# Attention values as the stationary operand, in two column halves of the array, with units handled in pairs

## What is computed

```python
# group A, for a block of 128 queries
s = (jnp.einsum('bqhd,bshd->bhqs', qn, k_nope)
     + jnp.einsum('bqhd,bsd->bhqs', qr, k_rope)).astype(jnp.float32) * scale
mask = (qp[:, None] // CHUNK) >= k_chunk[None, :]
s = jnp.where(mask[None, None], s, -jnp.inf)
p = jax.nn.softmax(s, axis=-1).astype(v.dtype)
return jnp.einsum('bhqs,bshd->bqhd', p, v)
...
# group B: the same with the keys of the top 256 of
rel = jax.nn.relu(jnp.einsum('bqhd,bsd->bqhs', iqb, ik).astype(jnp.float32))
score = jnp.einsum('bqh,bqhs->bqs', iwb.astype(jnp.float32) * w_scale, rel)
```

## Time and profile before

| | us |
|---|---|
| median of 3 runs | 4346.73 |
| lowest and highest | 4341.33, 4348.23 |
| profiled execution, its own time | 4354.86 |
| its span | 4352.8 |
| TensorE busy | 3868.6 (89%) |
| TensorE weight loads busy | 3113.4 (72%) |
| VectorE busy | 2261.7 (52%) |
| ScalarE busy | 1636.0 (38%) |
| GpSimd busy | 1351.6 (31%) |
| mean granted TensorE clock | 0.938 of full speed |

### The profile page before, as it was taken

One profiled execution on the slowest core, in us unless ns is written; L12 is line 12 of the kernel. 1 busy time (PEld: TensorE's weight loads), 2 busy tenths in 40 slices (PEclk: granted clock), 3 DMA queues, 4 the chain that ended last, 5 costly groups with the idle time before them and its releaser, 6 DMA issues. The chain is left out here.

```text
span 4352.8 us, 57519 instructions
## 1 busy us (share of the span) xinstructions
PE 3868.6 (89%) x20100; PEld 3113.4 (72%) x20100; DVE 2261.7 (52%) x4226; ACT 1636.0 (38%) x2907; POOL 1351.6 (31%) x845
## 2 busy tenths in 40 slices
PE   7999977778889899999895589699999999999998
PEld 5777744666677677777783467588878878879986
DVE  3222223899999898889942533244044224404421
ACT  3333323545556556555451222233133223213321
POOL 0000001555555455553001000144444444434332
PEclk9999988789999999899997689899999999999999
DMA  4222222101000000000001045533343433434331
GB/s 165 72 86 81 74 67 56 47 27 30 22 23 19 16 19 17 9 17 11 12 6 47 3 177 183 186 89 115 126 117 95 150 115 92 128 116 116 87 100 61
DMA packets 347675, 323.98 MB, mean 74 GB/s; under 512 B 52928, under 2 KB 284960, under 8 KB 347488
## 3 DMA queue, kind: packets, MB, share of 16 engines
q1 hardware_dynamic: 335360, 277.61, 21.7%
q10 hardware_dynamic: 7344, 26.74, 1.5%
q0 software_dynamic: 4800, 17.43, 1.0%
HBM read 251.54 MB, written 71.43 MB: 74 GB/s over the span
## 5 line engine op out<-in xcount | busy, mean ns | idle before, releaser
L1494 POOL TENSOR_TENSOR ff_w_lo<-ff_stage,ff_w_hi 128x2048 fp32r<-128x2048 f32 (+1 forms) x136 | 611.0, 4493 | 1212.6 <-ACT ff_w_hi L1576 1212.6
L2082 DVE TENSOR_SCALAR_CACHE_REDUCE at_hit<-at_score,at_su 128x384 bf16<-128x384 f32 (+13 forms) x434 | 641.1, 1477 | 8.6
L95 PE MATMUL ff_bank<-ff_h_hi,ff_w_hi 128*128 128x512 f32 (+1 forms) x1760 | 618.7, 352 | 29.7 <-DMA ff_h_lo<-scr_h2T 26.1
L96 PE MATMUL ff_bank<-ff_h_lo,ff_w_hi 128*128 128x512 f32 (+1 forms) x1760 | 620.4, 353 | 0.0
L97 PE MATMUL ff_bank<-ff_h_hi,ff_w_lo 128*128 128x512 f32 (+1 forms) x1760 | 619.2, 352 | 0.0
L1638 DVE TENSOR_TENSOR ff_a_lo<-ff_prod,ff_a_hi 128x512 f32 (+1 forms) x110 | 411.9, 3745 | 170.6 <-ACT ff_a_hi L1590 170.6
L1947 ACT ACTIVATE at_probt<-at_p_t 128x512 f32<-128x512 f32 (+3 forms) x640 | 321.1, 532 | 315.4 <-PE at_p_t L1881 314.1
L1576 ACT ACTIVATE ff_w_hi<-ff_stage 128x2048 fp32r<-128x2048 f32 (+1 forms) x136 | 253.2, 1862 | 443.0 <-PE ff_bank L97 416.2
L95 PEld LDWEIGHTS ff_bank<-ff_h_hi,ff_w_hi 128*128 128x128 f32 x1760 | 331.3, 188 | 79.6 <-issue 31.4
L1881 PE MATMUL at_p_t<-at_ident,at_prob 128*128 128x128 f32 x2176 | 337.2, 287 | 52.2 <-ACT at_prob L1938 51.8
L1938 ACT ACTIVATE at_prob<-at_prob,at_st 128x1024 f32<-128x1024 f32 (+7 forms) x384 | 341.9, 892 | 110.8 <-DVE at_st L2062 110.1
(11 more groups left out here) (253 smaller groups left out, 6608.6 us busy)
## 6 DMA issues: line engine op xcount, KB each, us to landing
ff_stage<-in_w_gate SPq DMA_DIRECT2D x88, 512.0 KB, 4.0
ff_stage<-in_w_up SPq DMA_DIRECT2D x88, 512.0 KB, 5.2
ff_stage<-in_w_down SPq DMA_DIRECT2D x40, 1024.0 KB, 5.1
pj_xt<-in_xT SPq DMA_DIRECT2D x17, 512.0 KB, 3.3
pj_x<-in_x SPq DMA_DIRECT2D x17, 512.0 KB, 4.4
scr_qT<-pj_qt SPq DMA_DIRECT2D x68, 128.0 KB, 2.3
mx_o<-scr_o SPq DMA_DIRECT2D x17, 512.0 KB, 7.0
mx_x<-in_x SPq DMA_DIRECT2D x17, 512.0 KB, 3.3
```

The costliest lines, as they stand in the source:

```text
L95: pe.matmul(out, lhs[0], rhs[0], start=start, stop=False)
L96: pe.matmul(out, lhs[0], rhs[1], start=False, stop=False)
L1494: pool.tensor_tensor(w_lo[a][:, 0:w], stage[a][:, 0:w], w_hi[a][:, 0:w].bitcast(F32), ALU.subtract).then_inc(s_wlo, 1)
L2082: step(dve.tensor_scalar(h_, s_, cand.bitcast(F32), 0.0, ALU.is_ge, ALU.add, cnt))
```

## The change

It swaps the two sides of the value product. The stationary side is now 64 columns of values (128 keys by 64), and the moving side is the 128 columns of transposed probabilities. Its result is 64 rows by 128 queries. Even key blocks write PSUM partitions 0 to 63, odd key blocks partitions 64 to 127 of `p_o[:, 0:128]`. When a head is done, ScalarE copies these 128x128 into `halves` (`take_halves`), and when eight heads are done, TensorE makes one product for each head (`fold_halves`), with the copied halves as stationary side and two stacked 64x64 identities, `fold`, as moving side. That adds the two halves and turns them back to queries by 64, over the whole bank `p_o`, which `take_values` evicts as before.

Units are handled in pairs: two are transposed, and then both are added. The first pair's transposes come before the second score chunk of the next slot. There is one `out` in place of two. Two small loads for `fold` are issued at the start.

```diff
+        self.blocks = self.W // P
+        self.pairs = [list(range(u, min(u + 2, self.U))) for u in range(0, self.U, 2)]
...
-        out = [m.sb(f"out{a}", [P, 512]) for a in range(2)]
-        ident = m.sb("ident", [P, P])
+        out = m.sb("out", [P, 512])
+        halves = m.sb("halves", [P, HA, P])
+        ident, fold = m.sb("ident", [P, P]), m.sb("fold", [P, VA])
...
+        t_half = tally("halves_taken", lambda t: H)
...
             sp.dma_start(ident[:, :], io["ident"]).then_inc(s_const, 16)
+            for half in range(2):
+                sp.dma_start(fold[half * VA:(half + 1) * VA, :], io["ident"][0:VA, 0:VA]).then_inc(s_const, 16)
...
-                if h % HA == 0 and u == 0:
+                if u == 0:
+                    t_half.wait(pe, n, h)
                     t_oev.wait(pe, n, h // HA)
...
-                    mm = pe.matmul(p_o[:, h % HA * VA:(h % HA + 1) * VA], probt[t_turn.at(n, f) % 2][:, b, :], vals,
-                                   start=blk == 0, stop=blk == t.W // P - 1)
+                    side = blk % 2 * VA
+                    mm = pe.matmul(p_o[side:side + VA, 0:P], vals, probt[t_turn.at(n, f) % 2][:, b, :],
+                                   start=blk < 2, stop=blk + 2 >= t.blocks)
                 mm.then_inc(t_pv.sem, 1)
+
+            def fold_halves(n, g):
+                t_half.wait(pe, n, (g + 1) * HA)
+                rows = min(2, tiles[n].blocks) * VA
+                for k in range(HA):
+                    mm = pe.matmul(p_o[:, k * VA:(k + 1) * VA], halves[0:rows, k, :], fold[0:rows, :], start=True, stop=True)
+                mm.then_inc(t_fold.sem, 1)
...
+                if nxt:
+                    product(*nxt, 0)
+                if s:
+                    for u in tiles[slots[s - 1][0]].pairs[-1]:
+                        add_values(*slots[s - 1], u)
+                for u in t.pairs[0]:
+                    turn(n, h, u)
+                if nxt and tiles[nxt[0]].C > 1:
+                    product(*nxt, 1)
+                if h % HA == 0 and s:
+                    fold_halves((s - 1) // H, (s - 1) % H // HA)
                 for q in index_units(s, 0):
                     index_unit(n + 2, q)
...
+                if t.U > 2:
+                    for u in t.pairs[0]:
+                        add_values(n, h, u)
+                    for u in t.pairs[1]:
+                        turn(n, h, u)
...
+            def take_halves(n, h):
+                t_pv.wait(act, n, (h + 1) * tiles[n].U)
+                t_fold.wait(act, n, h // HA)
+                rows = min(2, tiles[n].blocks) * VA
+                act.activation(halves[0:rows, h % HA, :], p_o[0:rows, 0:P], ACT.Copy).then_inc(t_half.sem, 1)
...
+                if s:
+                    take_halves(*slots[s - 1])
+                for u in t.pairs[0]:
+                    take(n, h, u)
                 if h % HA == 0 and s:
                     take_values((s - 1) // H, (s - 1) % H // HA)
```

More of the change, by code:

```diff
@@ L1768, in attend_prompt @@
         cand, miss = su[:, 0:1], su[:, 1:2]
-        s_const, s_zero, s_store = m.sem("const_in"), m.sem("tail_zeroed"), [m.sem(f"out{g}_stored") for g in range(2)]
+        s_const, s_zero, s_store = m.sem("const_in"), m.sem("tail_zeroed"), m.sem("out_stored")
         in_qa, in_qb, in_qi, in_iw = m.sem("qa_in"), m.sem("qb_in"), m.sem("qi_in"), m.sem("iw_in")
@@ L1844, in _ @@
             store(TP - 1, 1)
-            for g in range(2):
-                sp.wait_ge(s_store[g], 16 * TP)
+            sp.wait_ge(s_store, 16 * 2 * TP)
         @block.tensor
@@ L1915, in _ @@
                 t, nxt = tiles[n], after(s)
[L1916 to L1920 removed]
+                if nxt:
[9 more added lines that the diff above has]
+                    fold_halves((s - 1) // H, (s - 1) % H // HA)
                 for q in index_units(s, 0):
                     index_unit(n + 2, q)
[L1923 to L1926 removed]
+                if t.U > 2:
[3 more added lines that the diff above has]
+                        turn(n, h, u)
                 for q in index_units(s, 1):
                     index_unit(n + 2, q)
[L1929 removed]
+            for u in tiles[-1].pairs[-1]:
+                add_values(*slots[-1], u)
+            fold_halves(TP - 1, 1)
         @block.scalar
@@ L1975, in _ @@
                     relu(n + 2, q)
-                for u in range(tiles[n].U):
-                    take(n, h, u)
+                if t.U > 2:
+                    for u in t.pairs[1]:
+                        take(n, h, u)
                 for q in index_units(s, 1):
@@ L1985, in _ @@
                     exps(*nxt)
+            take_halves(*slots[-1])
             take_values(TP - 1, 1)
```

31 lines of the change are left out of this document (11 added, 20 removed).

## The result

| | before | changed |
|---|---|---|
| median of 7 runs each, us | 4346.73 | 4325.39 |
| lowest to highest, us | 4335.76 to 4359.34 | 4315.1 to 4336.22 |
| ratio, 95% interval | | 0.9948 [0.9928, 0.9967] |
| profiled execution: span, us | 4352.8 | 4334.2 |

The change makes the kernel 0.5% faster, 21 us where 41 were forecast. The time lies inside the range, 19 us above the forecast.

The account below looks back on a forecast made before the run. VectorE was taken to bound blocks 3 to 14 and TensorE block 15. The terms -22 (block 15), -32 (blocks 3 to 14), +12 (blocks 0 to 2) and +1 (loads) sum to -41, 4306 us as median; 8-in-10 range 4283 to 4366.

Parts of the forecast that it names:

- Passes and overlap: Value products on TensorE: a pass takes 0.060 us, between 0.055 with the column halves side by side and 0.110 without.
- Rival 1: Value products: the halves do not overlap, a pass stays at 0.110 us; +3 us, 4350 us; chance 0.20.
- rival 3: TensorE drains at each width change, 0.17 us four times a slot, halves not overlapping; +51 us, 4398 us; chance 0.13.
- The change of width: TensorE switching between full and narrower array, four times a slot: 0.0 us taken, 0.17 us as upper end.
- Block 15: Last query block, bound by TensorE: slots fall to 7.5 and 6.2 us, the end adds 2.5; net 22 us saved.
- the end: Very end of block 15: last copy, eight folds and semaphores come ahead of the eviction, adding 2.5 us.
- Blocks 3 to 14: Where VectorE is the bound: of 52.2 us of waits for score products, 32 us go.
- VectorE's work does not change: Assumption for VectorE: its work stays the same under the change; no term for it in the sum.
- wrong altogether: Sign against the whole forecast: VectorE's own steps in blocks 3 to 14 become longer, so the bound itself has moved.
- Blocks 0 to 2: Start of the attention: the copy ahead of ScalarE's eviction (7 us) and the exposed fold (5 us) cost 12 us.
- The +1 for the two loads: Start of the kernel: two more loads ahead of the mask all engines wait for, 0.42 us each, cost 1 us.
- Rival 2: Idle TensorE's clock falls to 1.2 GHz more often, so VectorE keeps nearly all waits; -13 us, 4334 us; chance 0.15.

Follow-up runs that it names:

- one-half version: Changed kernel with every key block in the same column half, so value passes do not overlap; 4372.91 us, ratio 1.0038.
- swap-only kernel: Changed kernel's products, copies and fold, but with the order of work of the kernel before; 4348.15 us, ratio 0.9982.
- order alone: Changed kernel's order in pairs with the value products of the kernel before, no halves, no fold; 4321.08 us, ratio 0.9926.
- the split: Changed kernel with GpSimd's two 128x1024 subtractions at each block's start cut into eight 128x128 pieces each; 4299.96 us, ratio 0.9884.
- the failed run: Changed kernel with GpSimd's subtractions in pieces, ScalarE copying halves behind the next exponential in blocks 0 to 7 except before folds; 4333.89 us, ratio 0.9963.
- the run that took ScalarE's wait for it away: Changed kernel with GpSimd's subtractions in pieces, ScalarE evicting the folded bank after the next exponentials in blocks 0 to 7; 4300.63 us, ratio 0.9885.

## Why the prediction was half right

**Passes and overlap: right.** 0.060 was taken, 0.055 measured, and 0.111 without the second half. Rival 1 falls, and with it rival 3 as it was priced, for that needed halves that do not overlap. The one-half version shows that rival 1, had it held, would have given 21 us over the kernel before and not 3. It gains nothing in blocks 3 to 14 (2.6 us longer), where 12 us were priced in for the order, and loses 11.1 us in block 15, where 2.5 were. The Trainium skill, "TensorE: Matmul & The Clock Gate", Part 3, has column-tiled matmuls run concurrently; these rows agree, with two halves at 2.0 times.

**The change of width: 0.0 taken, 0.14 and 0.04 us measured,** inside the bounds. It is wrong as a term: the four changes cost 0.36 us a slot, some 6 us over block 15, and the sign named for rival 3, a gap of over 0.1 us, is there at two changes in four, and at all of them in the swap-only kernel. Shorter passes (0.055 for 0.060 is 0.16 us a slot) paid for half of it. The Trainium skill, "TensorEngine Tiling (Array Packing)", Key Properties, has the engine drain at a change of mode. The 0.14 us agree in kind, though they are about half of a short pass's 0.27.

**Block 15: -22 forecast, -19.2 measured.** The slots came to 7.5 and 5.9 us (forecast 7.5 and 6.2). Those figures of the prediction included the fold, the measured ones don't: 16 x 1.66 = 26.6 us are saved in slots, and 7.4 us go for folds, the waits around them and the end, where 0.21 x 16 + 2.5 = 5.9 were forecast. The end was right (2.36 us). A fold inside the block was not: 2.68 us, of which the wait for the eviction, 0.78, had no place in the sum.

**Blocks 3 to 14: -32 forecast, -16.1 measured.** This is the term that was mis-sized. The sentence "of 52.2 us of waiting between 0 and 52 can go", with 32 taken, held for the waits: 31.2 us went. What failed is the step beside it, "VectorE's work does not change", by which its busy time was put at no change in the sum. The work stayed, but its own steps grew by 15.1 us. The prediction named this as what would make it "wrong altogether" but gave it no place in the sum and no chance. The cause is shown for most of it. With GpSimd's long instructions cut, the changed kernel has 4.5 us more VectorE time than the kernel before with the same cut (1176.8 and 1172.3), where it had 15.1 more without: 10.6 us came from which steps met the two subtractions. The other 4.5 us stay open. Some of it may be other GpSimd instructions, as in this place of the changed kernel's block 3, from the views of VectorE and of GpSimd, where a 0.29 us step ends 0.15 us behind one of 1.08 us:

```profile
898.04 1.01 DVE L2155 TENSOR_TENSOR at_chosen<-at_chosen,at_tail 128x128 bf16<-128x128 bf16 x1
```

```profile
897.82 1.08 POOL L2049 TENSOR_TENSOR at_rel<-at_rel,at_iws 128x512 f32<-128x512 f32 x1
```

**Who earned it: wrong.** The prediction gave the gain in blocks 3 to 14 to shorter passes, and to the order some 12 us. The order alone takes 26 us of the 31. Next to the order alone the swap pays in block 15, 12.3 us, and loses 11.7 us in blocks 0 to 2 and 5.0 in blocks 3 to 14. The direction was right, the reason for most of it was not the one given.

**Blocks 0 to 2: +12 forecast, +14.4 measured;** with the old products there and the split it is 7.5 us less. Of the two causes named, the copy's place is borne out by the trace and the failed run; the exposed fold stays open, since the run that took ScalarE's wait for it away gave TensorE one. The +1 for the two loads lies ahead of this stretch: the first minimum comes at 738.6 us instead of 738.3, and from 734.4 to 742.1 in the other runs, so no run shows it.

**Clock: right.** Rival 2 wanted a granted clock under 0.9 in blocks 5 to 14 and waits that stay; it was 0.94 there, and the waits went.

## What to carry to other kernels

Take apart a change that has an order and an arithmetic in it: here the order alone gave all the gain that the times can tell, and the new arithmetic paid only in the one block whose bound is TensorE (some 9 us by the length of block 15, too little for the medians to confirm), so use it there if at all. Where VectorE is the bound, its busy time is not a constant: list its elementwise steps by minimum and maximum, and wherever the maximum of one shape is several times the median, look for a long GpSimd instruction beside it and cut that in pieces. And a step moved out of one engine's way is only free if nothing on another engine waits for it with work queued behind.

## What the runs showed of the hardware

- A VectorE step of 128x128 that takes 0.29 us lasted up to 2.48 us beside a GpSimd subtraction of 2.35 us, and ended 0.14 us behind it where both are shown. With GpSimd's work cut into pieces of 0.46 us its maximum was 0.43 us. Steps that write an accumulator out kept their time beside one: the 374 of the search take 597.4 to 597.5 us in blocks 3 to 14, before, changed and with the split. VectorE in block 6 in order of time, and GpSimd's view of the same stretch:

```profile
1100.42 1.15 DVE L2138 TENSOR_SCALAR_CACHE_REDUCE at_chosen<-at_score,at_su 128x896 bf16<-128x896 f32 x1
...
1101.80 1.31 DVE L2142 TENSOR_SCALAR at_hit<-at_score,at_su 128x896 bf16<-128x896 f32 x1
```

```profile
1100.27 2.36 POOL L2033 TENSOR_TENSOR at_qi_lo<-at_qi_lo,at_qi_hi 128x1024 fp32r<-128x1024 f32 x1 [6.21 <-ACT at_qi_hi L1981]
```

  The first starts inside the subtraction and takes 1.15 us, as the search's steps of the same 896 columns do (1.144 on average over 31). The plain one behind it starts inside as well, takes 1.31 and ends 0.48 us behind GpSimd; at 768 and 1024 columns it takes 0.62 and 0.75 elsewhere. The Trainium skill, "SBUF — State Buffer", section "Who interferes with whom", has VectorE share a pair of ports with GpSimd, an exclusive lock: steps with two inputs in SBUF contend for it, and plain tensor_scalar can, in its two-port modes, but not the form that writes out its accumulator. The trace agrees with all three (lines 2155, 2142 and 2138).
- fp32 passes with 64 stationary columns start 0.055 us apart when they alternate between the two column halves, and 0.111 us apart in one half.
- A change from 64 to 128 stationary columns cost 0.14 us. One from 128 to 64 cost about 0.04 us behind the scores in the changed kernel, and 0.14 to 0.15 behind scores and transposes alike in the swap-only kernel.
- Removing 8.7 us from the busy time of the engine that looks like the bound moved the time by nothing measurable as long as it had 52 us of waits on another, and the same edit was worth 20 us or more once those waits were down to 21 to 26.
